# Forgetting-attention scores on TensorE: one four-byte float product against three passes over split q and k

## What is computed

```
q = heads(q) * (HEAD_DIM ** -0.5)
...
s = jnp.einsum('bhqd,bhkd->bhqk', qi, k).astype(jnp.float32)
s = s + ci[..., None] - c[:, :, None, :]
s = jnp.where(k_pos[None, :] <= q_pos[:, None], s, -jnp.inf)
p = jax.nn.softmax(s, axis=-1).astype(v.dtype)
return jnp.einsum('bhqk,bhkd->bhqd', p, v)
```

## Time and profile before

| | |
|---|---|
| median of 3 runs | 1529.75 us (1529.45 to 1530.89) |
| the profiled execution, its own time | 1529.32 us |
| its span | 1527.6 us |
| TensorE matmul busy | 1516.8 us (99%), 8892 records |
| VectorE busy | 991.9 us (65%) |
| ScalarE busy | 674.6 us (44%) |
| GpSimd busy | 385.2 us (25%) |
| granted TensorE clock, mean | 0.999 |

### The profile page before, as it was taken

How to read it: one execution, slowest core, us unless ns; L and a number is a source line. 1 busy time by engine, 2 the same in 40 slices (tenths; PEclk the granted TensorE clock), 3 DMA queues, 4 the chain that set the end, 5 groups by cost and what they waited for, 6 DMA issues and landing times.

```text
span 1527.6 us, 23066 instructions
## 1 busy us (share of the span) xinstructions
PE 1516.8 (99%) x8892; PEld 1336.4 (87%) x8892; DVE 991.9 (65%) x1429; ACT 674.6 (44%) x1109; POOL 385.2 (25%) x350
## 2 busy tenths in 40 slices
PE   9999999999999999999999999999999999999998
PEld 8878888888899999988898888888888999999886
DVE  4786677457588777673376979644446977777323
ACT  6224444323455454442286775332226554455221
POOL 3111004210112222288011802692012132221000
PEclk9999999999999999999999999999999999999999
DMA  7875113222432334355231212443232233334231
GB/s 219 302 252 165 56 56 84 97 83 83 147 102 79 93 106 111 113 178 165 83 98 56 83 56 70 133 150 117 82 109 60 80 111 105 93 108 140 95 110 55
DMA packets 188725, 171.40 MB, mean 112 GB/s; under 512 B 19793, under 2 KB 161105, under 8 KB 188625
## 3 DMA queue, kind: packets, MB, share of 16 engines
q1 hardware_dynamic: 181456, 144.84, 31.4%
q0 software_dynamic: 7168, 25.19, 4.9%
HBM read 167.91 MB, written 2.10 MB: 111 GB/s over the span
## 4 chain that ended last, share of the span: by engine, by line
PE 97%; DVE 1%; ACT 1%; issue 0%; DMA 0%; POOL 0%; SPq 0%; DVEq 0%; ACTq 0%; POOLq 0%
PE bank L2347 19%; PE bank L2349 19%; PE bank L2348 19%; PE bank L2441 8%; PE bank L2443 8%; PE bank L2442 8%; PE bank L2512 2%; PE bank L2513 2%; PE bank L2516 2%; PE bank L2663 1%; PE bank L2402 1%; PE bank L2415 1%; PE bank L2411 1%; PE bank L2573 1%; PE bank L2674 1%; PE bank L2707 0%
## 5 line engine op out<-in xcount | busy, mean ns | idle before, releaser
L1576 DVE TENSOR_TENSOR w_lo<-raw,w_hi 128x2048 fp32r<-128x2048 f32 (+1 forms) x109 | 211.5, 1941 | 215.4 <-ACT w_hi L1086 215.2
L2347 PE MATMUL bank<-h_hi,w_hi 128*128 128x512 f32 (+1 forms) x800 | 309.0, 386 | 0.0
L2349 PE MATMUL bank<-h_hi,w_lo 128*128 128x512 f32 (+1 forms) x800 | 298.6, 373 | 0.0
L2348 PE MATMUL bank<-h_lo,w_hi 128*128 128x512 f32 (+1 forms) x800 | 298.3, 373 | 0.0
L1086 ACT CAST w_hi<-raw 128x2048 fp32r<-128x2048 f32 (+1 forms) x108 | 171.4, 1587 | 200.0 <-PE bank L2349 194.4
L2347 PEld LDWEIGHTS bank<-h_hi,w_hi 128*128 128x128 f32 x800 | 150.9, 189 | 28.2 <-issue 1.9
L2348 PEld LDWEIGHTS bank<-h_lo,w_hi 128*128 128x128 f32 x800 | 151.0, 189 | 27.2 <-issue 1.9
L2349 PEld LDWEIGHTS bank<-h_hi,w_lo 128*128 128x128 f32 x800 | 150.7, 188 | 27.2
L2441 PE MATMUL bank<-s_hi,w_hi 128*128 128x256 f32 x576 | 163.3, 284 | 1.1 <-DVE act_m L1863 1.1
L2442 PE MATMUL bank<-s_lo,w_hi 128*128 128x256 f32 x576 | 163.1, 283 | 0.0
L2443 PE MATMUL bank<-s_hi,w_lo 128*128 128x256 f32 x576 | 163.1, 283 | 0.0
(11 more groups left out here) (493 smaller groups left out, 3213.0 us busy)
## 6 DMA issues: line engine op xcount, KB each, us to landing
raw<-in_w_in SPq DMA_DIRECT2D x102, 512.0 KB, 4.6
raw<-in_w_ffn_in SPq DMA_DIRECT2D x44, 512.0 KB, 5.0
mod_slabs<-in_mod_w POOLq DMA_DIRECT2D x16, 1024.0 KB, 6.0
raw<-in_w_gate SPq DMA_DIRECT2D x22, 512.0 KB, 4.0
raw<-in_w_up SPq DMA_DIRECT2D x22, 512.0 KB, 5.2
raw<-in_w_down SPq DMA_DIRECT2D x20, 512.0 KB, 4.6
raw<-in_w_ffn_out SPq DMA_DIRECT2D x20, 512.0 KB, 4.3
mod_raw<-in_mod_w POOLq DMA_DIRECT2D x32, 256.0 KB, 3.0
```

The source lines that it names most:

```text
L1576: ins = dve.tensor_tensor(w_lo[s][:, cols], raw[s][:, cols], w_hi[s][:, cols].bitcast(F32), ALU.subtract)
L2347: pe.matmul(o, st_hi, mv_hi, start=first, stop=False)
L2348: pe.matmul(o, st_hi, mv_lo, start=False, stop=False)
L2349: return pe.matmul(o, st_lo, mv_hi, start=False, stop=last)
```

## The change

ScalarE copies q and k of each head into `float32r` tensors (`q_hi`, `k_hi`, 2 KB per partition each, at places that other tensors leave free at that time). GpSimd subtracts these from q and k in place (`q_lo` lies where `q_t` lies, `k_lo` where `k_t` lies), in front of the mask of the same head, and TensorE makes the score as `three_passes`. The parts of head 0 are made ahead of the stage, those of head h + 1 in step i = 1 of head h. TensorE now waits for `masked_ready` at the first score of each head, since that semaphore is raised by the GpSimd instruction behind the two subtractions. A later count on `qk_hi_done`, in the second block, is raised by 8. The diff, with the waits:

```diff
+        q_lo = at("q_lo", A + 0, [P, HEADS, TOK], F32R)
+        k_lo = at("k_lo", A + 16, [P, HEADS, TOK], F32R)
+        hi_at = [(36, 38), (40, 42), (44, 46), (16, 18), (20, 52), (16, 18), (22, 24), (16, 18)]
+        q_hi, k_hi = ([at(f"{name}_hi{h}", A + kb[i], [P, TOK], F32R) for h, kb in enumerate(hi_at)] for i, name in enumerate("qk"))
...
             for h in range(HEADS):
+                gp.wait_ge(qk_hi_done, h + 1)
+                gp.tensor_tensor(q_lo[:, h, :], q_t[:, h, :], q_hi[h][:].bitcast(F32), ALU.subtract)
+                gp.tensor_tensor(k_lo[:, h, :], k_t[:, h, :], k_hi[h][:].bitcast(F32), ALU.subtract)
                 gp.wait_ge(c_kept, h + 1)
...
+            def qk_hi_part(h):
+                if h < 3:
+                    act.wait_ge(mod_summed, SLABS * len(EARLY))
+                else:
+                    act.wait_ge(score_ready, NT * (h - 1))
+                if h == 4:
+                    act.wait_ge(score_added, score_parts(NT * (h - 1)))
+                act.copy(q_hi[h][:], q_t[:, h, :])
+                act.copy(k_hi[h][:], k_t[:, h, :]).then_inc(qk_hi_done, 1)
...
+                if c == 1:
+                    for n in (n_q + 2, n_q + 3, n_k + 2, n_k + 3):
+                        wait_emptied(act, n, 1)
+                    qk_hi_part(0)
                 for t in range(NT):
                     take(n_va + 1, t, v_att[:, t, 512 * c:512 * c + 512], chunk_pace(c))
...
                 if i < 2:
                     split(n + 1, part=i)
+                if i == 1 and h + 1 < HEADS:
+                    qk_hi_part(h + 1)
...
-                    dve.wait_ge(qk_hi_done, 2 * j + f + 1)
+                    dve.wait_ge(qk_hi_done, HEADS + 2 * j + f + 1)
...
                     wait(pe, score_added, score_parts(s - 1))
-                    pe.matmul(bank[:, b, 0:w], q_t[:, h, P * i:P * i + P], k_t[:, h, 0:w], start=True, stop=True).then_inc(score_ready, 1)
+                    if i == 0:
+                        pe.wait_ge(masked_ready, h + 1)
+                    rows = slice(P * i, P * i + P)
+                    three_passes(bank[:, b, 0:w], q_hi[h][:, rows], q_lo[:, h, rows], k_hi[h][:, 0:w], k_lo[:, h, 0:w],
+                                 True, True).then_inc(score_ready, 1)
                     quarter(n_g + h, i)
```

## The result

The changed kernel takes 1536.18 us (median of 6 runs, 1535.20 to 1538.09) against 1529.78 (6 runs, 1529.36 to 1530.89) on the same chip: a ratio of 1.0041, 95% interval 1.0029 to 1.0054. It is slower by 6.4 us. Forecast were 1535.5, and slower with a chance of 0.63. The profiled span grew from 1527.6 to 1533.8 us.

The account below looks back on a forecast made before the run. TensorE, busy 1516.8 of 1527.6 us, was taken as the bound. Net loss of 0.75 us in seven heads (5.3), minus 0.3 in head 7, plus 1.0 for the tail gave +6.0: 1535.5 us, range 1527.2 to 1538.8.

Parts of the forecast that it names:

- the scaling at 1.18: VectorE's 384-column scaling in heads 0 to 6, held up by GpSimd's mask: 1.2 to 1.3 us in place of 0.42.
- the mask early by 0.58: GpSimd's mask ready 0.6 us before TensorE's first score of the next head, so the new wait costs nothing.
- both names in TensorE's waits: Sign: TensorE's waits name VectorE's 384-column scaling and the gate weights' low part, some 7 us in all.
- the distance of heads: Sign: from a head's first score to the next, growing from 16.2 to 16.9 us; 15.9 would mean no hold-up.
- passes, 8 heads: Attention scores on TensorE as three float32r passes instead of float32: 0.305 us saved per head, 2.4 over 8 heads.
- ScalarE's copies: Two added casts per head, 1.1 us, fit ScalarE's 1.92 us idle before `pt_hi`, leaving 0.6; cost nothing.
- three stalls: TensorE waits in heads 0 to 6 because GpSimd holds up VectorE: 0.33, 0.53 and 0.20, together 1.06 us per head.
- gates moved into head 7: About three pairs of GpSimd gate work move into head 7 and behind, meeting VectorE: 1.0 us, half of 2.1.
- the 384-key term: TensorE's score of 384 keys as three passes, each counted as 0.17 us: 0.18 us saved per head.
- The stall of i = 2: TensorE's transposes wait for VectorE's scaling of task i = 2, 0.9 us late behind GpSimd's mask: 0.33 us.
- The stall on the low part: TensorE's first gate quarter of the next head waits for VectorE's low part of the gate weights: 0.53 us.
- That of i = 3: TensorE's transposes wait for VectorE's scaling of task i = 3, ending at 199.58 instead of 198.68: 0.20 us.

Follow-up runs that it names:

- the signal to TensorE: The change with TensorE's wait at a head's first score released by the second subtraction, 1.3 us before the mask: 1535.70 us, ratio 1.0037.
- best version: The change with GpSimd's mask ahead of the subtractions, gates after the last head, gate weights' low parts at i = 0 and 1: 1527.05 us, ratio 0.9984.
- the same moves in float32: Kernel before, float32 scores and no parts, with GpSimd's gates after the last head and low parts at i = 0 and 1: 1528.81 us, ratio 0.9993.
- mask first: The change with GpSimd making the mask before it waits for the head's copies, so the two subtractions follow it: 1530.36 us, ratio 1.0002.
- gates later: The change with GpSimd's mask ahead of the subtractions and its gate work starting only when the last head is done: 1528.42 us, ratio 0.9989.

## Why the prediction was right, and where its sum was not

The mechanism is the one forecast, and its signs were there: passes 0.11 to 0.23 us apart (but for the first of each score, which takes 0.14 to 0.32), the scaling at 1.18 (forecast 1.2 to 1.3), the mask early by 0.58 (0.6), both names in TensorE's waits (with 4.3 us, not 7, on the matmuls), the distance of heads up to 16.8 (16.9). The runs bear it out: the work without the passes loses as much, another order of the same work takes the loss out of the heads, and the signal to TensorE does not matter. The total was 0.7 us off, and so close only because errors cancelled.

| term | forecast | measured, and from what |
|---|---|---|
| passes, 8 heads | -2.4 | -1.8 (best version against the same moves in float32) |
| ScalarE's copies | 0 | 0 (row below) |
| three stalls, 7 times 1.06 | +7.4 | +6.0 (7 times 0.86, from 16.80 against 15.94) |
| gates moved into head 7 | +1.0 | +1.7 to 2.1 (mask first against gates later, by the tail and by the medians) |
| sum | +6.0 | +5.9 to 6.3; the profiled span grew by 6.2, the median by 6.4 |

ScalarE's timeline in the changed kernel: 0.77 us of idle time is left ahead of `pt_hi`, of 1.92, where 0.6 was forecast, and the releaser is still TensorE.

```profile
193.21 0.37 ACT L1373 CAST pt_hi<-bank 128x256 fp32r<-128x256 f32 x1 [0.77 <-PE bank L2705]
```

- **The passes** saved less: the 384-key term, as above, 0.06 per head; the rest is a few hundredths. The Trainium skill (FP8 and Floating Point Precision, TensorE Precision Notes) counts four passes for a float32 product. By that page three for four would save 0.55 us per head, an estimate from the float32 scores' 2.22; 0.22 were measured, and the smallest size loses. A quarter of the 128-key score's 0.22 is 0.055, but a `float32r` pass of 128 columns takes 0.11. What sets the 0.11 no run here shows.
- **The stall of i = 2** was put at 0.33, and is 0.13 (0.36 from the last matmul to the transposes, less 0.23), with 0.06 more until the next score. The scaling came 0.76 late where 0.9 was forecast, and TensorE's head start was 0.28 (0.12 + 0.16), not 0.35. That accounts for all of the difference but a few hundredths.
- **The stall on the low part** was put at 0.53: the first quarter's score began at 196.89, its three passes would have ended 0.37 later, and the quarter began at 197.72, so 0.46. **That of i = 3** was put at 0.20 and measured 0.13 to 0.19. All three together are 0.86 for 1.06, against the best version; against the mask first, where VectorE's work has the order that it has in the change, they are 0.76.
- **Head 0** was counted like the others. There the scaling escaped (0.53 us) and the low part took the whole collision (2.31 us), and the distance to head 1 kept the passes' gain.
- **The tail** was the under-estimated term. One half of two times what a head loses was a choice between bounds, with no list of which instructions meet. A list would have shown it: the gate work runs without a pause from 263.66 to 284.33, across the scaling of 384 columns at 280.07 and the low part behind it. The forecast moved about three pairs into head 7; there are seven pairs in that stretch, and in the kernel before three start behind the first score of head 7.
- **The sum** of the measured terms is a rough one. The kernel before is itself 0.8 us longer than the float32 kernel with the same moves, from the first score of head 0 to the last product with v (135.55 against 134.74), and the table leaves that out. Between the same two points the changed kernel takes 141.42, which is 5.9 more.

In most of these kernels one distance of heads is 0.13 to 0.17 us longer than its neighbours (16.97 in the change, 16.17 with the mask first). The traces show where it begins: in every kernel with ScalarE's copies the exponential of 256 keys in head 3 starts 0.31 us after `pt_hi`, in every other head 0.16 or 0.17 (in the change 206.51 to 206.82), and the scaling behind it is as much later. In the best version it does not reach TensorE, whose distances in heads 1 to 6 all stay at 15.91 to 15.94. Why ScalarE starts late there stays open.

## What to carry to other kernels

An engine that shares a path with the one behind the critical engine is not free because it idles: look at which of its instructions will be running when the other's short, urgent one comes, and order them so that this one finds the path empty. When the critical engine gets faster, list first who is next to be waited for and by how much each is early; here slacks of 0.2 to 0.3 us, and a tail full of gate work, turned a gain of 1.8 us into a loss of 6.4, and putting the mask first, the gates later and the low parts earlier gave 3.1 below the kernel before. Where work is moved into a tail, write down each meeting instead of taking a share.

## What the runs showed of the hardware

- **Behind a GpSimd instruction with two inputs VectorE waits for its end.** In the changed kernel the scaling of 384 columns ends 0.21 to 0.23 us after the mask in heads 1 to 6, and in head 0 a low part that started 0.18 us after the mask took 2.31 for 1.22. Timelines of GpSimd and of VectorE there:

```profile
161.56 1.40 POOL L1020 TENSOR_TENSOR c_masked<-gate_a,mask_qk 128x512 f32<-128x512 f32 x1
```

```profile
161.74 2.31 DVE L1603 TENSOR_TENSOR w_lo<-raw,w_hi 128x1024 fp32r<-128x1024 f32 x1
```

  The Trainium skill (GPSIMD Engine Reference, Specifications) speaks of contention with VectorE instructions that have two SBUF inputs or run in a 2-port mode. The trace agrees for the low parts, which have two SBUF inputs; the scaling has one tensor input, and no run here shows in which mode it runs. The size of a meeting was up to 1.11 us (the scaling of 1.53 for 0.42), a little less than the GpSimd instruction of 1.29. That scaling's row even begins 0.03 us before GpSimd's (280.07 and 280.10), so where two rows begin this close they do not tell which one will wait.
- **Behind GpSimd's gate plus one, which has one input, VectorE loses less.** The low part of 281.53 above started 0.17 us after such a gate and took 1.62 for 1.22, 0.40 more, where behind the mask it lost 1.09:

```profile
281.36 1.60 POOL L1024 TENSOR_SCALAR gate_a<-gate_a 128x512 f32<-128x512 f32 x1
```

  In the kernel before, a scaling of 512 columns that started 0.39 us after a gate (246.83 after 246.44, with 1.50 us of gate) took 0.50, as one takes without (0.49). So what a move of GpSimd's work costs depends on which instruction meets which, and not only on how long GpSimd is busy.
- **VectorE instructions that read PSUM or reduce were not held up.** GpSimd's product ran from 265.35 to 266.64 in the changed kernel, and on VectorE stood:

```profile
265.37 0.55 DVE L1983 TENSOR_TENSOR prob<-bank,gate_a 128x384 f32<-128x384 f32 x1
265.84 0.28 DVE L1986 TENSOR_TENSOR prob<-bank,c_masked 128x128 f32<-128x128 f32 x1
266.15 0.69 DVE L1988 TENSOR_REDUCE neg_max<-prob 128x1 f32<-128x512 f32 x1
```

  the times that the same forms have with GpSimd idle (0.55, 0.28, 0.69 from 197.59 on). I had not expected the reduction, with its input in SBUF, among them.
- **A 128-column pass takes 0.11 us behind another of its size** (197.03 to 197.14), half of the 0.23 of 512 columns and not a quarter, so splitting the float32 product of 128 columns into three cost 0.15 us here.
